# Input tiles in another order with the scan's preparation between them, and expert token rows fetched by an indirect DMA

## The reference

```
h = RMSNorm(x) * (1 + scale1) + shift1
u = h @ w_in        # conv 512 | Fourier 256 | RWKV-7 1920 | three gates 3072 columns
x += gate1 * (sum_b sigmoid(gate_b) * branch_b) @ w_o
h = RMSNorm(x) * (1 + scale2) + shift2
x += gate2 * FFN(h) # layer 0: dense SwiGLU; layer 1: top-2 of 8 experts, 1408 wide
```

## Time and profile before

| what | value |
|---|---|
| median of three runs | 1881.76 us (1878.26 to 1881.91) |
| the profiled execution's own time | 1884.37 us |
| its span, first to last instruction | 1882.6 us |
| mean granted TensorE clock | 0.974 of full speed |
| busy: TensorE, VectorE, ScalarE, GpSimd | 1767.0 (94%), 1133.7 (60%), 903.8 (48%), 555.2 (29%) |
| chain that ended last | TensorE 79%, VectorE 10%, issue 4%, ScalarE 4%, DMA 2% |
| DMA | 315 MB, 167 GB/s over the span |

### The profile page before, as it was taken

The page is one execution under the profiler, slowest core; times in us unless marked ns, Lnnn a source line. Parts: engine busy times, 40 slices in busy tenths (PEclk is TensorE's granted clock), DMA queues, the critical chain, the costliest instruction groups (busy, mean ns, idle before and its releaser), DMA issues.

```text
span 1882.6 us, 40983 instructions
## 1 busy us (share of the span) xinstructions
PE 1767.0 (94%) x16558; PEld 1622.9 (86%) x16558; DVE 1133.7 (60%) x1623; ACT 903.8 (48%) x1358; POOL 555.2 (29%) x423
## 2 busy tenths in 40 slices
PE   7998888999999999999979889999999999999996
PEld 6996868899999999989878788999788888888885
DVE  2466687654231111035656886532689988889988
ACT  3444142343353443243532424344577767777765
POOL 1650000355566666657500004566200000000000
PEclk9999989999999999989989899999899999999998
DMA  9456222233434434424562002337399899999980
GB/s 318 142 160 224 75 84 73 87 112 129 142 94 124 122 119 141 127 76 129 184 198 82 5 4 60 112 126 252 108 315 316 292 309 304 314 314 318 297 281 34
DMA packets 225157, 315.32 MB, mean 167 GB/s; under 512 B 15606, under 2 KB 169588, under 8 KB 224884
## 3 DMA queue, kind: packets, MB, share of 16 engines
q1 hardware_dynamic: 220112, 308.26, 50.5%
q10 hardware_dynamic: 4900, 4.93, 0.8%
HBM read 311.05 MB, written 2.10 MB: 166 GB/s over the span
## 4 chain that ended last, share of the span: by engine, by line
PE 79%; DVE 10%; issue 4%; ACT 4%; DMA 2%; DVEq 0%; POOL 0%; SPq 0%; ACTq 0%
PE bank L621 77%; PE bank L618 2%; DVE e_w_rest L187 2%; DMA ring<-in_w_ada 2%; DVE S L2035 2%; ACT e_w_rounded L1409 1%; DVE cvT L1938 1%; DVE U L2065 0%; DVE St L2087 0%; DVE tmp L1953 0%; DVE St L2084 0%; DVE ey_rest L2354 0%; POOL sq L2445 0%; DVE hT L1807 0%; DVE inv L2044 0%
## 5 line engine op out<-in xcount | busy, mean ns | idle before, releaser
L2437 POOL TENSOR_TENSOR weights_rest<-ring,weights_rounded 128x512 fp32r<-128x512 f32 x344 | 466.3, 1359 | 435.0 <-ACT weights_rounded L1372 433.9
L187 DVE TENSOR_TENSOR e_w_rest<-e_raw,e_w_rounded 128x1024 fp32r<-128x1024 f32 (+1 forms) x326 | 353.7, 1131 | 35.2 <-ACT e_w_rounded L1409 33.9
L1372 ACT ACTIVATE weights_rounded<-ring 128x512 fp32r<-128x512 f32 x344 | 215.2, 629 | 317.8 <-PE bank L621 311.3
L1409 ACT ACTIVATE e_w_rounded<-e_raw 128x1024 fp32r<-128x1024 f32 (+1 forms) x327 | 315.5, 989 | 78.9 <-PE bank L621 78.1
L621 PE MATMUL bank<-h_rounded,weights_rounded 128*128 128x384 f32 x688 | 230.9, 336 | 2.1 <-DVE h_rest L1839 1.7
L621 PE MATMUL bank<-h_rounded,weights_rest 128*128 128x384 f32 x688 | 229.9, 334 | 0.0
L621 PE MATMUL bank<-h_rest,weights_rounded 128*128 128x384 f32 x688 | 229.9, 334 | 0.0
L621 PE MATMUL bank<-e_w_rounded,hG_rounded 128*128 128x512 f32 (+1 forms) x432 | 164.4, 381 | 5.1 <-DVE e_w_rest L187 3.4
L621 PE MATMUL bank<-e_w_rest,hG_rounded 128*128 128x512 f32 (+1 forms) x432 | 162.8, 377 | 0.0
L621 PE MATMUL bank<-e_w_rounded,hG_rest 128*128 128x512 f32 (+1 forms) x432 | 162.8, 377 | 0.0
L621 PE MATMUL bank<-hg_rounded,weights_rounded 128*128 128x384 f32 x384 | 129.7, 338 | 3.6 <-DVE hg_rest L1839 3.6
(11 more groups left out here) (350 smaller groups left out, 3616.5 us busy)
## 6 DMA issues: line engine op xcount, KB each, us to landing
ring<-in_w_ada SPq DMA_DIRECT2D x96, 512.0 KB, 5.9
e_raw<-in_moe_w_down SPq DMA_DIRECT2D x90, 512.0 KB, 4.7
ring<-in_w_in SPq DMA_DIRECT2D x88, 512.0 KB, 4.7
e_raw<-in_moe_w_gate SPq DMA_DIRECT2D x72, 512.0 KB, 5.8
e_raw<-in_moe_w_up SPq DMA_DIRECT2D x72, 512.0 KB, 7.0
e_raw<-in_moe_w_gate SPq DMA_DIRECT2D x36, 384.0 KB, 3.9
e_raw<-in_moe_w_up SPq DMA_DIRECT2D x36, 384.0 KB, 4.0
ring<-in_ffn_w_gate SPq DMA_DIRECT2D x22, 512.0 KB, 4.7
```

Of the source, the lines that this page charges most:

```text
L187: eng.tensor_tensor(wl, e_raw[n % E_RAW][:, 0:kn * w], wr.bitcast(F32), ALU.subtract).then_inc(s("e_rest"), 1)
L1372: a(w_parts[n % NSLOT][0], raw, ACT.Copy).then_inc(*E.up("rounded_ready", *key))
L1409: a(e_w[n % E_PARTS][0][:, 0:kn * w], e_raw[n % E_RAW][:, 0:kn * w], ACT.Copy).then_inc(s("e_rounded"), 1)
L2437: pool.tensor_tensor(wl, raw, wr.bitcast(F32), ALU.subtract).then_inc(*E.up("rest_ready", *key))
```

## The change

*Input tiles.* The order of z is 12, 13, 14, 4 to 7, 0 to 3, 8 to 11, in the blocks, the pieces and the tiles alike. After chosen tiles, each engine gets a part of the preparation: on TensorE after tile 6 the four products of the decay, after 8 those of the rate, after 12 the key norms, after 15 their spreading (banks 4 to 7 for all); on ScalarE the matching sigmoids, gains, squares, root and exponentials; on VectorE mixing of 3, 4, 4 and 4 tiles with the parts between. The keys are multiplied by `key_products` and `first_keys`; transposes wait for `keys_ready`, the pairs for `ark_ready`. `ksq`, `shifted`, `gain` and `conv_b` move in memory. The halves before direction 0 become 1+2; the start of direction 1 has 6, its steps 2 each, the last step 2. Copies, turning and making of the second modulation move behind the first gate tiles.

*Experts.* Before the loop GpSimd adds the two parts of the token rows and stores them in DRAM (`h_rows`, three DMAs of 512 KB). `sel` and `wsel` of the next job are made before piece 20's rest. `wsel` gets a second column with the token's number, so `slot_rows` (three products of two columns, after piece 20) yields weight and row number; VectorE copies both (`slot_values`), GpSimd issues one indirect DMA of 128 rows x 4 KB into `hgt`, and TensorE waits for it (`e_rows_in`) after piece 31. The gather in the loop and ScalarE's copies go; the first job keeps its own.

```diff
+Z_ORDER = (12, 13, 14, 4, 5, 6, 7, 0, 1, 2, 3, 8, 9, 10, 11)
-GATHER_AT, GATHERED_AT = 29, 31
+SELECT_AT, SLOTS_AT, ROWS_AT, GATHERED_AT = 20, 20, 25, 31
...
-                meanwhile(2)
-                b = begin("kks", l)
...
-                lowrank(0)
-                meanwhile(1)
...
+                behind = {6: decays, 8: rates, 12: key_norms, 15: key_scales}
+                tiles = [("z", l, m) for m in Z_ORDER] + [("cf", l, m) for m in range(6)]
+                dense_two(tiles[:2], "z", l)
+                for n, job in enumerate(tiles[2:], 2):
+                    dense(job, "z", l)
+                    if n in behind:
+                        behind[n]()
...
-                meanwhile(5)
+                meanwhile(2)
...
-                        ada_turn(l, (1, 2))
-                        meanwhile(2)
-                    pe.wait_ge(*at("ark_ready", l, d))
+                        meanwhile(6)
+                    pe.wait_ge(*at("keys_ready", l, d))
...
-                            meanwhile(1)
+                            meanwhile(2)
...
-                            meanwhile(2 if d == 0 else 1)
+                            meanwhile(2)
...
-                between_tiles = {(0, 1): lambda: conv_norm(1), (1, 1): turned_y, (1, 3): bonus, (1, 4): output_gate}
+                between_tiles = {(0, 1): lambda: conv_norm(1), (0, 2): lambda: ada_turn(l, (1, 2)), (1, 1): turned_y, (1, 3): bonus, (1, 4): output_gate}
...
+            def slot_rows(i):
+
+                pe.wait_ge(s("e_wsel"), i + 1)
                 for j in range(3):
-                    last = mm(psum[5][:, 0:1], sel[:, j, :].bitcast(F32), wsel[:, j:j + 1], j == 0, j == 2)
-                last.then_inc(s("e_selT_full"), 1)
+                    last = mm(psum[2][:, 0:2], sel[:, j, :].bitcast(F32), wsel[:, j, :], j == 0, j == 2)
+                last.then_inc(s("e_slot_full"), 1)
...
-                    if n == GATHER_AT:
-                        pe.wait_ge(s("e_sel"), i + 2)
-                        for h in range(2):
-                            for part in range(2):
-                                gather(h, part)
-                    elif n == GATHERED_AT:
-                        turn_gathered(i + 1)
+                    if n == GATHERED_AT:
+                        pe.wait_ge(s("e_rows_in"), i * 16 + 16)
+                        turn_gathered(False)
...
+                behind = {5: low_inputs, 7: lambda: low_sigmoids(0, 0, range(NM)), 9: lambda: low_sigmoids(0, 1, range(NM)),
+                          10: gains, 11: key_squares, 13: key_roots, 14: first_exps, 16: lambda: (second_exp(), third_exp())}
...
+                mix_tiles(12, 3, "mix_low")
+                mix_tiles(4, 4)
+                key_parts()
...
+                decay_sums()
+                mix_tiles(0, 4)
+                key_reciprocal()
+                mix_tiles(8, 4)
+                key_products()
+                gated_conv()
...
+                    if c == 2:
+                        e_rests(i, done, SELECT_AT)
+                        dve.wait_ge(s("e_selT_full"), i + 1)
...
+                        select_weights(lambda at_: bass.ds(code + at_, 1)).then_inc(s("e_wsel"), 1)
+                        e_rests(i, SELECT_AT, ROWS_AT)
+                        dve.wait_ge(s("e_selT"), i * 2 + 2)
+                        slot_values(i + 1)
...
+            for j in range(3):
+                pool.tensor_tensor(h_sums[:, j, :], hT_parts[0][:, j, :].bitcast(F32), hT_parts[1][:, j, :].bitcast(F32), ALU.add)\
+                    .then_inc(*E.up("row_summed"))
+                pool.wait_ge(*at("row_summed"))
+                pool.dma_start(h_rows[j * P:(j + 1) * P, :], h_sums[:, j, :]).then_inc(*E.up("rows_stored", by=16))
...
+            with pool.Fori(0, njobs) as i:
+                pool.wait_ge(s("e_rows_at"), i + 2)
+                pool.wait_ge(s("e_hT_full"), i * 2 + 2)
+                pool.sem_inc(s("e_rows_go"), 1)
+                pool.indirect_dma_start(hgt, None, h_rows, bass.IndirectOffsetOnAxis(rows_at, 0))\
+                    .then_inc(s("e_rows_in"), 16)
```

More of the change, by code:

```diff
@@ L299, in build @@
         assert at_("z") + 2 * KD * T <= used["cvT"][1]
+        assert used["fno_z"][1] <= at_("shifted") and used["shifted"][1] <= at_("gain") and used["gain"][1] <= at_("conv_b")
         NSLOT = 3
@@ L817, in low_product, with decays @@
                         .then_inc(*E.fill("low", l, d, which, m))
[L819 to L825, removed]
-                lowrank(0)
-                meanwhile(1)
[L829 to L834, removed]
+                def decays():
+                    pe.wait_ge(*at("low_in", l))
+                    pe.wait_ge(*at("low_in_ready", l))
+                    for m in range(NM):
+                        low_product(0, 0, m, use=4 + m)
@@ new lines, in rates, with key_norms @@
+                def rates():
+                    for m in range(NM):
+                        low_product(0, 1, m, use=4 + m)
+                def key_norms():
+                    if l == 0:
+                        pe.wait_ge(*at("second_in"))
+                    b = begin("kks", l, use=7)
+                    pe.wait_ge(*at("ksq_ready", l))
+                    some = heads[:, 48:80]
+                    for m in range(NM):
+                        last = mm(b[32 * m:32 * m + 32, 0:T], some, ksq[:, m, :], True, True)
+                    last.then_inc(*E.fill("kks", l))
@@ L843, in _ @@
                     last.then_inc(*E.fill("fno1", l, j))
+                for m in range(NM):
+                    pe.wait_ge(*drained("kkn", l, m))
                 meanwhile(1)
@@ L1495, in exps, with low_inputs, gains @@
-                def exps(d):
-                    act.wait_ge(*at("L_ready", l, d))
-                    L = L3(d)
+                def low_inputs():
+                    act.wait_ge(*at("mix_low", l))
+                    a(z[:, 12, :], z[:, 12, :], ACT.Sigmoid).then_inc(*E.up("act_step"))
+                    a(z[:, 13, :], z[:, 13, :], ACT.Tanh).then_inc(*E.up("low_in_ready", l))
+                def gains():
+                    for m in range(NM):
+                        act.wait_ge(*drained("low", l, 0, 1, m))
+                    key_gain(0)
@@ new lines, in key_products @@
+                def key_products():
+                    for m in range(NM):
+                        dve.wait_ge(*filled("kkn", l, m))
+                        tt(kk[:, m, :], kk[:, m, :], bank("kkn", l, m)[:, 0:T], M).then_inc(*E.read("kkn", l, m))
+                    for m in range(NM):
+                        dve.wait_ge(*drained("kkn", l, m))
+                    dve.wait_ge(*at("BK_gain", l, 0))
+                    tt(v3(tmp4[1]), kk, v3(tmp4[1]), M).then_inc(*E.step())
+                    tt(v3(gain), v3(gain), k_, M).then_inc(*E.step())
```

306 lines of the change are left out of this document (152 added, 154 removed).

## The result

The change makes the kernel faster by 1%: **1863.15 us**, median of 4 runs (1855.54 to 1873.32), against 1881.84 for the kernel before in the same batch (4 runs, 1878.26 to 1886.0). The ratio is 0.9903, 95% interval [0.9876, 0.9931]. I had forecast 1846 (1826 to 1868): the direction and the range held, but 35.3 us were forecast and 18.7 came.

The account below looks back on a forecast made before the run. TensorE, busy 94%, was taken as the bound, VectorE second in the experts' jobs. Layers -18.6, fetch -20.7, start of experts +4 gave -35.3 us: 1846, own range 1836 to 1857, wide range 1826 to 1868.

Parts of the forecast that it names:

- 2.7 plus 0.8 for coincidences: Tile stage, per layer: 2.7 us of preparation inserts left uncovered, plus 0.8 for coincidences (bounds 0 and 6).
- The six halves' +2.5: Start of the second direction: six half-chunks of the next modulation there wait for weights, +2.5 us (bounds 0 and 4).
- the ring: Modulation weights: the ring holds three halves; the fourth comes 7 us after the first is used, the next 2.9 later.
- The four more in the steps: Second direction's steps: four more halves mostly replace idle time, +0.8 us in layer 0, nothing in layer 1.
- The last tile then ends at 144.2: Layer 0's tile stage: 133.46 plus 7.2 of inserts plus 3.5 of stalls; scan transposes then start at 155.1, 13.5 us earlier.
- Net -2.3 per job: Experts: twelve products (2.80 us) leave each job, two costs of 0.25 come back; -20.7 us for nine jobs.
- The two quarters: Each expert job: +0.25 us for VectorE and +0.25 for a short stand at piece 20, whose selection comes in front.
- The gates' +1.3: Gates: the modulation's eight transposes move there, +1.0 us, and 0.3 for two bank copies of ScalarE.
- The squeeze of the tile stage: Rival: ScalarE and GpSimd fall behind, TensorE waits on the rests; some 4 of 18.6 us remain, 1861; chance 0.12.
- The fetch taking VectorE's time: Rival, experts: the fetch's issue holds VectorE off for one piece, each job gives back 1.2, +11, 1857; chance 0.10.
- the rows coming late: Rival, experts: rows land 6 to 7.5 us later, TensorE waits about 6.3 after piece 31; +21, 1903; chance 0.08.
- the weights' stream as the bound: Rival, experts: the weights' DMA becomes the bound, jobs keep 56 us, 1867; chance 0.02.

Follow-up runs that it names:

- its shifted version: Kernel before with 4 unused columns of zeros in its first table, moving everything behind by 16 bytes: 1891.8 us, ratio 1.0063.
- the two fetch-only kernels: Kernel before with only the change's fetch half: 1871.53 us, ratio 0.9921, with 4 columns in the token table; 1861.4 us, 0.9885, with 16.
- tiles-only: Kernel before with everything of the change except the fetch (tile order, preparation between tiles, halves' new places): 1874.5 us, ratio 0.996.
- table of 16: The changed kernel with the new token table 16 columns wide instead of 4, a shift of 64 bytes instead of 16: 1852.1 us, ratio 0.9845.
- table of 8: The changed kernel with the new token table 8 columns wide instead of 4, a shift of 32 bytes: 1857.61 us, ratio 0.9856.
- after again: The changed kernel, unchanged, run once more: 1862.8 us, ratio 0.9879 to the kernel before.
- steps as before: Changed kernel with 16 token-table columns and the third exponential one tile later, plus the halves within the steps as in before: 1850.08 us, ratio 0.9829.

## Why the prediction was right, and where it was not

Segments read from TensorE's timeline, each from the first product of one kind to that of the next, in us. "Code before" is the range over before, its shifted version and the two fetch-only kernels; "changed" is tiles-only, table of 16 and table of 8 (without the 175.5 ns), for the scans also after again. Each kernel has one profiled execution.

| segment | code before | changed | difference forecast | found |
|---|---|---|---|---|
| first tile to scan transposes, layer 0 | 123.7, 124.2 (without the 175.5 ns) | 111.9 to 112.8 | -13.5 | -10.9 to -12.3 |
| the same, layer 1 | 122.8, 123.1 (the same) | 112.7 | -13.5 | -10.1 to -10.4 |
| start of 2nd direction, layer 0 | 13.5 to 13.7 | 16.1 to 16.9 | +2.5 | +3 |
| the same, layer 1 | 13.1 to 13.3 | 16.1 to 17.3 | +2.5 | +3 to +4 |
| 1st direction, layer 0 | 83.8 to 87.0 | 88.4 to 88.9 | +0.8 | +3 |
| 2nd direction, layer 0 | 80.6 to 83.6 | 85.8 to 90.5 | (with it) | +6 |
| 1st direction, layer 1 | 84.7 to 92.8 | 81.5 to 83.6 | 0 | -5 |
| 2nd direction, layer 1 | 76.8 to 77.1 | 78.5 to 81.6 | 0 | +2.5 |
| gates to router, layer 1 | 195.1 to 195.3 | 192.9 | +1.3 | -2.3 |
| router to first expert product | 10.7 (15.6 with fetch) | 15.7 | +4 | +5.0 |
| one job | 56.1 | 52.95 (table of 16), 53.42 (of 8), 53.25 (after) | -2.3 | -2.7 to -3.1 |

*What held.* The mechanism of the tiles: the transposes start behind nothing, the Fourier stretch took 10.20 us where my sum had 10.3, and the waits for rests behind the inserts (0.24, 0.28, 0.16, 0.20 and 1.83 in after again) make 2.7, where I had 2.7 plus 0.8 for coincidences. The 1.83 is above the 1.5 that I had named as the most for one tile. The six halves' +2.5 is nearly right in layer 0, for the reason given, the ring. The fetch's rows are hidden: 12 us were forecast between request and use, 12.3 passed. GpSimd's additions hold VectorE off once each, +4 forecast, +5.0 found; moving them removed the stand. TensorE's 7.2 us of inserts came to 7.85.

*What failed, by its step.*
1. **No term for the place of the data: some 10 us, the largest single miss.** The sum costed instructions and waits, and took "the same products" to last as long. The diff's new table of 4 columns moved their operands by 16 bytes: 8.5 us in the layers by the segments, 9.9 for the whole kernel before. With the table of 16 the change gives 1852.1, 6 from the forecast and inside its own range of 1836 to 1857. The measured 1863 lies outside that range, and within 1826 to 1868 only because the wide range was opened for the rivals.
2. **"The four more in the steps mostly replace idle time: +0.8, and nothing in layer 1".** Found for the second direction, where the four more stand: +6 in layer 0 and +2.5 in layer 1. In layer 0 some of it is shown to go with the halves (4.0 us less with the steps as before, against one execution). They come with waits for their blocks in some kernels (6.3 us at 328.6 in the chain of tiles-only; none in before's second direction), and with a lowered clock in others (0.71 and 0.60 at 310 to 330 in after again). How the rest divides stays open. The first directions have the same steps in both kernels and changed too, for which I had no term: +3 in layer 0, not explained, and -5 in layer 1, where the wait for the halves' weights ahead of it is gone (7.3 us, a clock of 0.76 behind it in before). That it is the clock is read from these windows, not tested.
3. **"The last tile then ends at 144.2", 13.5 us earlier.** Some 2 us short in layer 0 and 3 in layer 1. The waits were sized right; the lower clock behind the 1.83 (in most executions) and the inserts' 0.65 were not in the sum. Counted as I had put it, the stage to the last tile took 101.6 us in after, at the edge of the 102 that I had named as the mark of a wrong forecast.
4. **"Net -2.3 per job".** The two quarters that I added, for VectorE and for a stand at piece 20, did not appear: in after a job lost 2.8, just the twelve products of 2.80. With the table of 16 it lost 3.1, the 0.3 more being faster products (230.3 ns instead of 232.0), which no term of mine had either. With nine jobs this is 4 to 7 us better than my term, and hides part of the misses above; that is luck.

One reading ahead of the sum was wrong too: "only about 20 us of work" in the 35.1 behind the tiles. The works that I listed there add up to 24.6 (14.6, and ten halves at 1.0). The sum did not use it.

The sum with what was found: by the medians of the kernels with the table of 16, the fetch gives 20.4 (forecast 16.7, start included), the tiles 9.3 (forecast 18.6), and the table of 4 in its place takes 11 (forecast nothing): 18.7 again. The gates' +1.3 shows as +0.9, from the first gate tile to the first product of `merged` (143.3 to 144.2 us in layer 0, 142.9 to 143.8 in layer 1). The norm behind took it back: in layer 1 it kept its clock (0.83 for 20 us in before, 1.00 with the change), which makes the -2.3 of the table.

*The rivals.* The squeeze of the tile stage (1861) comes near by its time, but not by its mechanism: the tiles' part was halved, by the steps at least as much as by the tile stage. The fetch taking VectorE's time, the rows coming late and the weights' stream as the bound did not happen; the stream ran at 340 GB/s in a job. The rule of the Trainium skill (SBUF — State Buffer, "SBUF: two separate sides") spoke against a DMA issued by GpSimd beside a busy VectorE. Here nine of them took 1.5 us each and landed after 4.7 to 8.5, with VectorE busy in 53.4 of 56 us; nothing of the starving was seen. The page speaks of VectorE operations in a 2-port mode; whether VectorE's pieces here run in one, no run shows. Its lock between computing operations agrees with the 2.38 and 2.92 us above.

## What to carry to other kernels

When a diff adds a constant or a buffer ahead of others, work out where everything behind it comes to lie, and compare the spacing of products in code that the diff does not touch: that one reading found the largest missing term here, and padding the table repaid 11 us by the medians. Work that filled a wait is not free once the wait is gone: ask for each filler where it goes, whether its data are there, and what the clock does behind the new wait. Price a stage over several kernels that share its code; one profiled execution had 27 us at half clock that the next had not.

## What the runs showed of the hardware

- TensorE's 128x384 products with both operands at a multiple of 32 bytes per partition follow each other every 173.4 ns, with all of it 16 bytes further every 175.5, in every stage of both layers; the kernel before slows by 0.6% for it.
- The experts' products of 128x512, which stream weights from a fixed column: 232.0 ns in before, 232.5, 233.3 and 230.3 in the changed kernel with shifts of 16, 32 and 64 bytes; jobs of 53.25, 53.42 and 52.95 us. What decides it is not explained.
- Runs of one kernel spread with the granted clock: after took 1873.3, 1863.9, 1862.5 and 1855.5 us at mean clocks of 0.971, 0.976, 0.977 and 0.980.
- A VectorE operation on 16 columns (0.18 us in before) took 2.92 us beside an addition of GpSimd; moved by one wait, the same additions cost 2.4 us less in sum.
